# A hybrid attention and mixture-of-experts block: the first norm moved from rows to transposed columns

## What is computed

```python
h = rms_norm(x, g_mix)                      # x * rsqrt(mean(x*x) + 1e-6) * g_mix
proj = h @ w_in                             # 1024 x 9728: q, k, v of 3 attention groups, retention, gates
...                                         # dilated attention, retention, gated merge
x = x + merged @ w_out
h2 = rms_norm(x, g_ffn)
y = hier_moe(h2, ...)                       # top-1 of 4 groups, top-2 of its 8 experts, SwiGLU
x = x + y
return rms_norm(x, g_final)
```

## Time and profile before

| | |
|---|---|
| Median of 3 runs | 791.28 us (790.79 to 791.46) |
| Profiled execution, its own time | 790.88 us |
| Its span in the trace | 789.1 us |
| PE busy, share of the span | 581.5 us, 74% |
| DVE busy | 248.5 us, 31% |
| ACT busy | 195.5 us, 25% |
| POOL busy | 13.4 us, 2% |
| HBM read | 254.45 MB, mean 324 GB/s |

### The profile page before, as it was taken

One profiled execution on the slowest core, in us unless ns is written; L12 is line 12 of the kernel. 1 busy time (PEld: TensorE's weight loads), 2 busy tenths in 40 slices (PEclk: granted clock), 3 DMA queues, 4 the chain that ended last, 5 costly groups with the idle time before them and its releaser, 6 DMA issues.

```text
span 789.1 us, 11609 instructions
## 1 busy us (share of the span) xinstructions
PE 581.5 (74%) x4469; PEld 413.2 (52%) x4469; DVE 248.5 (31%) x435; ACT 195.5 (25%) x292; POOL 13.4 (2%) x28
## 2 busy tenths in 40 slices
PE   3999999999999999976690590690690690690695
PEld 2999999999999998862230230230230230320231
DVE  5776685766664455571000000000000000000001
ACT  5354553666545443320000000000000000000002
POOL 3000000000000000010000000000000000000000
PEclk9999999999999999978695795696695795795699
DMA  8758658365686555899999999999999999999995
GB/s 237 229 159 263 183 177 259 90 172 161 168 242 186 186 180 191 338 412 392 424 429 429 424 429 427 425 429 429 425 429 426 425 429 429 426 429 427 425 417 210
DMA packets 94200, 255.85 MB, mean 324 GB/s; under 512 B 8800, under 2 KB 70240, under 8 KB 81888
## 3 DMA queue, kind: packets, MB, share of 16 engines
q1 hardware_dynamic: 91952, 255.35, 84.4%
q10 hardware_dynamic: 2224, 0.17, 0.2%
HBM read 254.45 MB, written 1.05 MB: 324 GB/s over the span
## 4 chain that ended last, share of the span: by engine, by line
PE 66%; DMA 29%; DVE 2%; ACT 1%; SPq 1%; issue 1%; POOLq 0%; POOL 0%; DVEq 0%; ACTq 0%
PE ps L1085 65%; DMA ring<-in_w_down 28%; DMA gain<-in_g_mix 1%; ACT work L604 1%; DVE hn L744 1%; SPq L483 0%; DVE work L925 0%; PE ps L1167 0%; PE ps L1191 0%; DVE hT L752 0%; DVE split L723 0%; DVE hn L1063 0%; ACT hn L663 0%; SPq L355 0%; DVE work L1002 0%
## 5 line engine op out<-in xcount | busy, mean ns | idle before, releaser
L1085 PE MATMUL ps<-store,work 128*32 128x512 f32 x128 | 71.7, 722 | 175.7 <-DMA ring<-in_w_down 175.1
L1085 PE MATMUL ps<-ring,work 128*32 128x512 f32 x896 | 184.6, 612 | 1.6 <-DVE work L1002 0.9
L723 DVE TENSOR_TENSOR split<-ring,split 128x768 fp32r<-128x768 f32 (+2 forms) x132 | 120.7, 932 | 92.4 <-ACT split L559 92.0
L1085 PE MATMUL ps<-hT,split 128*128 128x256 f32 x1152 | 141.9, 285 | 1.9 <-DVE hT L752 1.9
L1085 PEld LDWEIGHTS ps<-hT,split 128*128 128x128 f32 x1152 | 140.3, 193 | 2.9 <-issue 2.9
L559 ACT ACTIVATE split<-ring 128x768 fp32r<-128x768 f32 (+2 forms) x132 | 107.3, 825 | 123.1 <-PE ps L1085 93.8
L1085 PEld LDWEIGHTS ps<-store,work 128*32 128x32 f32 x128 | 15.6, 130 | 224.1 <-DMA ring<-in_w_down 164.4
L1085 PE MATMUL ps<-split,hT 128*128 128x256 f32 (+2 forms) x672 | 106.6, 316 | 0.0
L1085 PEld LDWEIGHTS ps<-split,hT 128*128 128x128 f32 x672 | 98.1, 190 | 4.9 <-issue 0.5
L1002 DVE COPY work<-ps 128x512 f32<-128x512 f32 x8 | 5.5, 692 | 254.8 <-PE ps L1085 254.8
L1085 PE MATMUL ps<-hT_slot,work 128*32 128x512 f32 x128 | 71.7, 722 | 0.0
(11 more groups left out here) (180 smaller groups left out, 460.2 us busy)
## 6 DMA issues: line engine op xcount, KB each, us to landing
ring<-in_w_up SPq DMA_DIRECT2D x24, 2048.0 KB, 34.6
ring<-in_w_gate SPq DMA_DIRECT2D x18, 2048.0 KB, 25.1
ring<-in_w_in SPq DMA_DIRECT2D x96, 192.0 KB, 4.1
mid<-in_w_up SPq DMA_DIRECT2D x8, 2048.0 KB, 34.3
oRT_slot<-in_w_down SPq DMA_DIRECT2D x7, 2048.0 KB, 26.4
store<-in_w_down SPq DMA_DIRECT2D x7, 2048.0 KB, 17.5
hT_slot<-in_w_down SPq DMA_DIRECT2D x7, 2048.0 KB, 21.9
ring<-in_w_in SPq DMA_DIRECT2D x96, 128.0 KB, 2.4
```

What stands on the lines that cost most here:

```text
L723: dve.tensor_tensor(split[:, s, 1, 0:n], raw(s, n), split[:, s, 0, 0:n].bitcast(F32), ALU.subtract).then_inc(lo_ready, 1)
L1085: return pe.matmul(o, lhsT=l, rhs=r, start=start, stop=stop, skip_group_check=shared)
```

## The change

1. PE transposes the raw rows of x as each half lands (`transpose_rows(t)`, L1123 of the changed kernel), reading them with a step of 8 elements; DVE no longer writes `hn` for the first norm.
2. The roots become a table. DVE multiplies the identity with each root (`spread`), PE multiplies a matrix of ones with it, so that every partition holds the roots of all 256 tokens; DVE copies that to `roots`.
3. DVE norms the transposed columns out of PSUM: 8 instructions of 128x256 (`norm_columns`), transposed value x g_mix (as a per-partition scalar, `mix_k`, 4 KB, loaded by ACT's queue) x root. ACT and DVE split the result in 4 parts (`normed_high`, `normed_low`), woven into the first quad's splits; PE waits for part s ahead of chunk s.
4. PE runs 16 matmuls identity x identity into a bank that nobody reads (`unread`): 6 ahead, 2 between the halves, 8 behind the table of roots.
5. `bias_t` is built in three pieces inside pair 0: behind the second and the fourth key split and behind the first value split. To place them, pair 0 leaves the loop.
6. POOL builds all its tables first and takes the two roots behind them.
7. The broadcast load of g_mix is gone; g_ffn goes to that buffer behind the loads of the fourth pair; the router's weights and bias are loaded from ACT's queue behind the first quad's splits, not ahead of everything.

```diff
@@ sync @@
             for t in range(TT):
                 sp.dma_start(xs[:, t, :], x_v[:, t, :]).then_inc(s_x[t], 16)
-            sp.dma_start(gain[:, :], g_mix.partition_broadcast(P)).then_inc(s_gain, 16)
...
             with sp.Fori(1, PAIRS) as i:
                 load_pair(i)
+            sp.dma_start(gain[:, :], g_ffn.partition_broadcast(P)).then_inc(s_gain, 16)
...
-            sp.wait_ge(hn_done, TT)
-            sp.dma_start(gain[:, :], g_ffn.partition_broadcast(P)).then_inc(s_gain, 16)
@@ gpsimd @@
-            pool.wait_ge(const_ready, 2)
-            inv_root(0)
-
             pool.iota(dist_i[:, :], pattern=[[1, T]], base=-P, channel_multiplier=-1).then_inc(const_ready, 1)
...
+            pool.wait_ge(const_ready, 2)
+            inv_root(0)
             with pool.Fori(0, RET_HEADS) as i:
@@ scalar @@
-            act.dma_start(wr[:, :, :], w_router.rearrange("(k p) n -> p k n", p=P)).then_inc(s_wr, 16)
-            act.dma_start(br[:, :], b_router.partition_broadcast(P)).then_inc(s_wr, 16)
+            act.dma_start(mix_k[:, :], g_mix.rearrange("(p k) -> p k", k=KT)).then_inc(s_mix, 16)
...
+            def normed_high(m):
+                act.wait_ge(normed_done, 2 * m + 2)
+                act.activation(hT[:, 0, 2 * m:2 * m + 2, :], normed[:, 2 * m:2 * m + 2, :], ACT.Copy).then_inc(hT_act, 1)
 
             high(0, 0, W_A)
+            normed_high(0)
+            normed_high(1)
             high(0, 1, W_A)
-            transposed_high(0)
-            transposed_high(1)
+            normed_high(2)
             high(0, 2, W_A)
+            normed_high(3)
             high(0, 3, W_A)
 
+            act.dma_start(wr[:, :, :], w_router.rearrange("(k p) n -> p k n", p=P)).then_inc(s_wr, 16)
+            act.dma_start(br[:, :], b_router.partition_broadcast(P)).then_inc(s_wr, 16)
@@ vector @@
-            mean_square(0)
-            dve.wait_ge(s_gain, 16)
-            for t in range(TT):
+            dve.memset(all_ones, 1.0).then_inc(ones_done, 1)
+            dve.wait_ge(const_ready, 1)
+            for t in range(TT):
+                dve.wait_ge(sq_done, t + 1)
+                dve.tensor_scalar(ms[:, 0, t:t + 1], ss[:, 0, t:t + 1], 1.0 / D, EPS, ALU.mult, ALU.add).then_inc(ms_done, 1)
                 dve.wait_ge(rstd_done, t + 1)
-                dve.scalar_tensor_tensor(hn[:, t, :, :], permuted(xs[:, t, :]), rstd[:, 0, t:t + 1], permuted(gain[:, :]),
-                                         ALU.mult, ALU.mult).then_inc(hn_done, 1)
...
+                dve.tensor_scalar(spread[:, t, :], ident[:, :], rstd[:, 0, t:t + 1], None, ALU.mult).then_inc(spread_done, 1)
+            dve.wait_ge(roots_psum, 1)
+            dve.tensor_copy(roots, bank(4, T)).then_inc(roots_ev, 1)
...
+            def norm_columns(m):
+
+                dve.wait_ge(hT_psum, 3 if m < 2 else 4)
+                for k in (2 * m, 2 * m + 1):
+                    dve.scalar_tensor_tensor(normed[:, k, :], ps[:, k // 2, (k % 2) * T:(k % 2 + 1) * T], mix_k[:, k:k + 1],
+                                             roots, ALU.mult, ALU.mult).then_inc(normed_done, 1)
...
+            norm_columns(0)
+            norm_columns(1)
             low(0, 0, W_A)
+            normed_low(0)
+            normed_low(1)
             low(0, 1, W_A)
-            transposed_low(0)
-            transposed_low(1)
+            norm_columns(2)
+            norm_columns(3)
+            normed_low(2)
             low(0, 2, W_A)
+            normed_low(3)
             low(0, 3, W_A)
...
             def attention(i, n_next):
                 for s in range(CH):
                     low(3 * i + 1, s, W_A)
+                    if isinstance(i, int) and i == 0 and s % 2 == 1:
+                        bias_of(s // 2)
                 for s in range(CH):
+                    if isinstance(i, int) and i == 0 and s == 1:
+                        bias_of(2)
...
-            with dve.Fori(0, PAIRS - 1) as i:
+            attention(0, W_A)
+            with dve.Fori(1, PAIRS - 1) as i:
                 attention(i, W_A)
@@ tensor @@
+            def unread(n):
+
+                for _i in range(n):
+                    mm(ps[:, 7, 0:P], ident[:, :], ident[:, :], True, True)
...
+            unread(6)
             transpose_rows(0)
-
-            pe.wait_ge(hT_dve, 2 * TT - 1)
+            unread(2)
+            transpose_rows(1)
+            pe.wait_ge(ones_done, 1)
+            for t in range(TT):
+                pe.wait_ge(spread_done, t + 1)
+                ins = mm(ps[:, 4, t * P:(t + 1) * P], all_ones, spread[:, t, :], True, True)
+            ins.then_inc(roots_psum, 1)
+            unread(8)
 
             with pe.Fori(0, PAIRS) as i:
                 queries = columns(NG, 0, W_A)
-                quad(3 * i, W_A, 2, queries, range(2))
-                pe.wait_ge(hT_dve, 2 * TT)
-                quad(3 * i, W_A, 2, queries, range(2, CH))
+                for s in range(CH):
+                    pe.wait_ge(hT_dve, s + 1)
+                    quad(3 * i, W_A, 2, queries, range(s, s + 1))
```

More of the change, by code:

```diff
@@ L134, in hybrid_block @@
         gain_k = sb("gain_k", [P, KT])
+        mix_k = sb("mix_k", [P, KT])
         bias_t = sb("bias_t", [P, NG, T])
@@ L175, in hybrid_block @@
         dist = take(T)
+        all_ones = take(P)
+        spread = take(T).rearrange("p (a q) -> p a q", a=TT)
+        roots = take(T)
+        normed = hn[:, :, :, :].rearrange("p a k q -> p (a k q)").rearrange("p (k t) -> p k t", k=KT)
         take = carve([0])
@@ L243, in hybrid_block @@
         s_gk = sem("s_gk")
+        s_mix = sem("s_mix")
+        ones_done, spread_done, roots_psum, roots_ev, normed_done = (sem("ones_done"), sem("spread_done"), sem("roots_psum"),
+                                                                     sem("roots_ev"), sem("normed_done"))
         wr_ready = sem("wr_ready")
@@ L747, in transposed_low @@
-            def transposed_low(t):
-                for h in range(2):
-                    b = 2 * t + h
-                    dve.wait_ge(hT_act, b + 1)
-                    steps, tokens = slice(4 * h, 4 * h + 4), slice(t * P, (t + 1) * P)
-                    dve.tensor_tensor(hT[:, 1, steps, tokens], ps[:, b, :].rearrange("p (k t) -> p k t", k=4),
-                                      hT[:, 0, steps, tokens].bitcast(F32), ALU.subtract).then_inc(hT_dve, 1)
+                dve.tensor_scalar(spread[:, t, :], ident[:, :], rstd[:, 0, t:t + 1], None, ALU.mult).then_inc(spread_done, 1)
@@ L759, in _, with bias_of @@
+            norm_columns(3)
+            normed_low(2)
             low(0, 2, W_A)
+            normed_low(3)
             low(0, 3, W_A)
-            dve.wait_ge(const_ready, 3)
-            link(dve.tensor_copy(dist, dist_i))
-            for g, (window, dil) in enumerate(GROUPS):
+            def bias_of(g):
+                window, dil = GROUPS[g]
+                if g == 0:
+                    dve.wait_ge(const_ready, 3)
+                    link(dve.tensor_copy(dist, dist_i))
                 link(dve.tensor_single_scalar(resid_i, dist_i, dil - 1, ALU.bitwise_and))
@@ L1091, in mm3, with transpose_rows @@
                 return mm(o, l[1], r[0], False, False, True)
-            def transpose_rows(n):
-                for t in range(TT):
-                    pe.wait_ge(hn_done, TT * n + t + 1)
-                    for k in range(KT):
-                        ins = pe.transpose(ps[:, 2 * t + k // 4, (k % 4) * P:(k % 4 + 1) * P], hn[:, t, k, :],
-                                           ident[:, :])
-                        if k in (3, 7):
-                            ins.then_inc(hT_psum, 1)
+            def unread(n):
+                for _i in range(n):
+                    mm(ps[:, 7, 0:P], ident[:, :], ident[:, :], True, True)
+            def transpose_rows(t):
+                pe.wait_ge(s_x[t], 16)
+                rows_t = xs[:, t, :].rearrange("q (p k) -> q k p", k=KT)
+                for k in range(KT):
+                    at = (k % 2) * T + t * P
+                    ins = pe.transpose(ps[:, k // 2, at:at + P], rows_t[:, k, :], ident[:, :])
+                    if k in (3, 7):
+                        ins.then_inc(hT_psum, 1)
             def quad(Q, n, steps, use, chunks=range(CH)):
```

24 lines of the change are left out of this document (10 added, 14 removed).

## The result

The changed kernel takes **784.75 us** (median of 6 runs, 783.44 to 787.43), the kernel before beside it 791.44 (6 runs, 790.79 to 791.99): 0.9917 of it, 95% interval 0.9905 to 0.9929. The profiled executions are 785.37 us (span 783.6) and 790.88 (789.1), 5.5 us apart.

A forecast was written before the change was run, and what follows sets the result against it. PE bounds up to the projections' end, then the expert stream. 4.1 us at the start plus 1.5 of clock, less 2.1 for the distances, gives 3.5 us: 787.8 us, 45 in 100, range 786.3 to 790.5.

The forecast's parts named there:

- What bounds: Up to the projections' end PE bounds; a microsecond PE gets there earlier starts the expert stream, and ends it, one earlier.
- The chain that replaces the gain's load: At the start, roots, norms and splits on DVE replace the gain's load; PE starts at 13.0 us, not 17.1.
- The column norms: DVE's eight 128x256 instructions out of PSUM, 0.47 us each or 0.43 start to start; first four from 9.7 to 11.4.
- The three pieces of distances: On DVE's list before the scores, pieces of 3.0, 1.9 and 1.9 us; they take back 2.1 us of 5.6.
- The loads of g_ffn at nothing: The g_ffn load, moved near 130 us and away from near 313 us, costs and gives nothing.
- Dear transposes: Rival, 10 in 100: PE's step-8 transposes cost 0.37 us each (bounds 0.21 to 0.37), losing 2.0 us: 789.8 us.
- The clock falls in the new wait: Rival, 20 in 100: PE's clock halves behind its 1.8 us stand before the scores, costing 1.5 us: 789.3 us.
- DVE has a list without a gap: DVE busy from 20.5 to 33.6 us, its keys' copy starting at 32.7; PE stands 1.8, scores begin at 33.7.
- The roots at 9.3: Before the first column norms, the roots' table passes PE and PSUM by 9.3 us, second root out at 8.4.
- DVE is ahead: Rival, 10 in 100: quicker POOL tables or distances fitting gaps let PE alone set the scores; gain 5.2 us, 786.1 us.
- From the scores on both lists are as before: Behind the scores PE's and DVE's lists stay unchanged, so the 3.5 us gained there is the whole sum.
- The unread matmuls cost nothing, and what they keep is hidden too: PE's unread matmuls fall into waits; the 1.5 us of clock they keep is hidden behind the keys' copy.

The follow-up runs named there:

- no_unread: The changed kernel with its three calls of unread matmuls taken out; 786.12 us, 0.9915 of the kernel before.
- warm: The changed kernel with 16 unread matmuls instead of 8 behind the table of roots; 784.5 us, 0.9915 of the kernel before.
- gffn_late: The changed kernel with g_ffn loaded behind all projection loads, ahead of the experts'; 785.59 us, 0.9924 of the kernel before.
- roots_first: The changed kernel with POOL's roots ahead of its tables, as in the kernel before; 784.76 us, 0.991 of the kernel before.
- router_early: The changed kernel with the router's two loads first on ACT's queue again; 785.12 us, 0.9918 of the kernel before.
- early012_warm: As early0_warm, with the second and third pieces of distances behind the third and fourth key splits; 784.56 us, 0.9906 of the kernel before.
- early0_warm: The changed kernel with 16 unread matmuls, first distances piece before the first root, POOL's roots ahead of its last tables; 784.23 us, 0.9906 of the kernel before.
- before_unread: The kernel before with eight unread matmuls between its transposes and its first projection matmul; 791.4 us, 0.9991 of the kernel before.
- before_again: The kernel before, unchanged, run once more for a second trace; 791.55 us, 1.0003 of the kernel before.
- after: The changed kernel itself, in its first measurement and profile; 784.75 us, 0.9917 of the kernel before.

## Why the prediction was wrong, and where it was right

**Right.** What bounds (PE to the scores, and an early microsecond of PE is one at the end): in all of these profiles the time from the scores to the end stayed between 750 and 754 us while the scores moved by 7.5, and the part of it up to the end of the projections stayed at 295.1 or 295.3. The chain that replaces the gain's load. The column norms, 1.66 for four. The three pieces of distances, predicted 3.0, 1.9 and 1.9: they ran from 20.79 to 23.80, from 25.55 to 27.44 and from 28.32 to 30.22. The loads of g_ffn at nothing. Dear transposes fell: 8 with a step of 8 elements took 1.04 us in the second half, 0.13 each, below the lower bound, and the unread matmuls without a step took 0.12 each (16 in 1.95). Their weight loads take 188 ns, those of the unread ones 192, so no cost of the step shows on PE, and the 72 ns that the prediction read from the earlier trace rows as the price of a step of 4 had another cause, which stays open. The 0.21 of the lower bound is a price at the half rate: in `no_unread`, whose projections start at that rate, the 16 transposes with a step take 3.65 us, 0.22 each. The Trainium skill (SBUF — State Buffer, Door 1: The DMA port swizzle, its note on cachelines) would make such reads dear; DVE's rows agree, PE's transposes do not. "The clock falls in the new wait" fell in `warm`, `gffn_late` and `roots_first`, where that wait exists. That it falls behind about 2 us of standing held in five of seven executions with that wait at the first projection matmul.

**Wrong: the sum, 3.5 us for 6.7.** Three terms of it failed; the second is part of the first.

1. *"DVE has a list without a gap", the copy at 32.7.* From the first key split on DVE the list was right: predicted 20.5 to 33.6, 13.1 us; measured 19.04 to 32.31, 13.3. But I had its start 1.5 us too late, and with it the scores (33.7; 32.36). Of this, 0.7 is the start of PE and DVE. The rest is ACT: its last split of the first quad ended at 17.05 us, not 18.2, and I had counted its three DMA issues as time of the engine. Its queue issued them from 15.22 to 16.74 us while it computed (the rows at 15.65 to 16.28 above), and the first key split was out at 19.03 instead of 20.5.
2. *The roots at 9.3.* The table was there at 8.49. I had taken POOL's tables at 5.1 us; they took 2.6, from 1.51 to 4.12, since the 5.1 held 2.6 us in which two of them stood beside DVE's norm of rows (last section). But that alone was not it (`roots_first`): the second half of x landed earlier because the router's two loads no longer went ahead, and `router_early` gives the 13.0 back. It is worth 0.7 us at PE's start, the same 0.7 as above, and this is what made the rival "DVE is ahead" nearly true.
3. *"From the scores on both lists are as before": the layout, 1.3 us, which was in no term and in no rival.* The change adds a tile of 32 bytes for a reason of its own, and with it the two long stages behind the scores were faster: by 0.2 us in the projections and 1.1 in the stream of experts.

Two errors hid each other in the profile: I had counted the clock as kept, and it was lost, behind the wait of 2.04. PE therefore ended its key quad at 31.15 and not at 29.90, as in `gffn_late`, and the wait for the copy, 1.01 us there where I had put 1.8, became the clock's loss ahead of it. The scores differ by 0.24 us between the two. In total: 4.8 to 5.6 us at the scores by the two pairs of profiles, and 1.3 by the layout, is 6.1 to 6.9; 6.7 was measured, and 5.7 (0.9928) with the tile moved behind the others.

"The unread matmuls cost nothing, and what they keep is hidden too" was wrong as well: without them the table of roots is 0.3 us later (8.81) and the clock stays low for longer, 0.8 us at the scores.

What stays open: the stage between the projections and the first down array took 29.8 to 32.5 us over the nineteen profiles, in part by where the clock stood (the router's 32 matmuls, 5.09 us in the chain of before, took 3.7 to 5.5); the rest was not traced. This hides smaller steps: `early012_warm` is 1.1 us ahead of the changed kernel at the scores, took 32.5 us here where that took 29.8, and is level with it at the end. The fastest version that was run is `early0_warm`, 784.23 us, not told apart from the changed kernel by its interval.

## What to carry to other kernels

When two engines' lists meet at one point, price each against the other before adding gains: here the earlier start of PE and the later distances are worth nothing alone and 5 us together, and an experiment that undoes only one of them would call either useless. Take each term's start from what will be true after the change (loads that no longer go ahead, engines that no longer disturb), not from the trace of before. And a change that adds a small tile moves every tile behind it: allocate that tile alone as an experiment before explaining what a distant stage gained.

## What the runs showed of the hardware

**POOL's selects and roots are held while DVE norms rows from SBUF to SBUF** (an instruction with two inputs in SBUF). The same selects in `before_unread`, the first just ahead of DVE's norm of rows and the second beside it (the norm runs from 9.76 us):

```profile
9.56 0.29 POOL L528 TENSOR_SCALAR_AFFINE_SELECT before<-before 128x128 bf16<-128x128 bf16 x1
...
10.69 1.19 POOL L538 TENSOR_SCALAR_AFFINE_SELECT ident_b<-ident_b 8x8 bf16<-8x8 bf16 x1
```

The second ends at 11.88 us, about where the first of the two norms does (4.12 us for both). In the kernel before, where both lay beside it, they took 1.90 and 1.12; in the changed kernel 0.29 and 0.18. Beside DVE's norms out of PSUM they are not held: `roots_first` has them at 9.05 and 10.18 us, with 0.29 and 0.18, against my expectation. A root of POOL beside the second norm, 331.7 us, takes 2.41 instead of 0.55.

**32 bytes of layout** are worth 1.1 us of 425.7 in a stream that keeps the DMA engines 0.99 busy.

**The clock's state at the start varies between executions of one kernel**: `before_again` worked at half rate for 5.7 us from its first projection matmul, the first profile for 3.4 us from 18.4, which is 0.9 us at the scores. The granted clock of the trace reads 1.00 in that stretch of `before_again`, though its matmuls are 0.22 us apart; their count shows the rate. And with one list on PE and one wait of 2.04 us ahead, the clock fell in `after` and was kept in `gffn_late`.

**DMA issues on ACT's queue lie beside ACT's own work**: in the changed kernel three issues from 15.22 to 16.74 us, while ACT splits and copies.
